# Hybrid attention layer: in its second attention half, three PSUM banks for scores and three for transposes, in place of two and four

## What is computed

```python
rel = jax.nn.relu(jnp.einsum('bqhd,bkd->bqhk', qib, k_idx) * (D_IDX ** -0.5))
score = jnp.einsum('bqhk,bqh->bqk', rel, wib)
score = jnp.where((s[None, :] <= t[:, None])[None], score, -jnp.inf)
_, idx = lax.top_k(score, k_top)
...
logits = jnp.einsum('bqhd,bqkhd->bhqk', qb, kg) * (D_HEAD ** -0.5)
logits = jnp.where(sel_ok[:, None], logits, -jnp.inf)
p = jax.nn.softmax(logits, axis=-1)
return jnp.einsum('bhqk,bqkhd->bqhd', p, vg)
```

## Time and profile before

| | us |
|---|---|
| median of 3 executions | 1729.43 |
| lowest, highest | 1728.17, 1732.9 |
| the profiled execution | 1732.58 |
| its span, first to last instruction | 1730.8 |

### The profile page before, as it was taken

One profiled execution on the slowest core, in us unless ns is written; L12 is line 12 of the kernel. 1 busy time (PEld: TensorE's weight loads), 2 busy tenths in 40 slices (PEclk: granted clock), 3 DMA queues, 4 the chain that ended last, 5 costly groups with the idle time before them and its releaser, 6 DMA issues. The chain is left out here.

```text
span 1730.8 us, 23456 instructions
## 1 busy us (share of the span) xinstructions
PE 1633.7 (94%) x8360; PEld 1376.5 (80%) x8360; DVE 1240.2 (72%) x1966; ACT 853.1 (49%) x1650; POOL 546.6 (32%) x332
## 2 busy tenths in 40 slices
PE   5999999999999999988889999899999989999997
PEld 5899888799877777777768878688888878888885
DVE  6287798898988989688863445874554458777878
ACT  5366455455445545577751243655555543333334
POOL 1111245555435435321103450675555500000000
PEclk9999999999999999999989999999999999999998
DMA  4565424344333233356304352233444365443544
GB/s 177 171 184 152 123 94 141 114 127 114 95 101 107 93 106 107 102 126 135 87 28 156 134 183 98 97 140 140 164 168 159 118 237 201 158 170 122 171 140 103
DMA packets 101372, 231.23 MB, mean 134 GB/s; under 512 B 11192, under 2 KB 25848, under 8 KB 101256
## 3 DMA queue, kind: packets, MB, share of 16 engines
q1 hardware_dynamic: 100680, 227.64, 41.2%
q0 software_dynamic: 576, 2.10, 0.7%
HBM read 155.83 MB, written 73.86 MB: 133 GB/s over the span
## 5 line engine op out<-in xcount | busy, mean ns | idle before, releaser
L727 PE MATMUL pj<-x_hi,w_hi 128*128 128x512 f32 (+2 forms) x816 | 304.0, 373 | 1.8 <-DVE rp_t L1031 1.8
L727 PE MATMUL pj<-x_lo,w_hi 128*128 128x512 f32 (+2 forms) x816 | 294.0, 360 | 0.0
L727 PE MATMUL pj<-x_hi,w_lo 128*128 128x512 f32 (+2 forms) x816 | 293.9, 360 | 0.0
L683 POOL TENSOR_TENSOR pt_lo<-a_buf,pt_hi 128x512 fp32r<-128x512 f32 (+3 forms) x104 | 137.5, 1338 | 191.0 <-ACT pt_hi L948 191.0
L336 POOL TENSOR_TENSOR w_lo<-w_raw,w_hi 128x1024 fp32r<-128x1024 f32 x53 | 132.9, 2507 | 183.7 <-ACT w_hi L332 183.6
L1105 DVE TENSOR_SCALAR_CACHE_REDUCE counted<-sc,small 128x272 uint8<-128x272 f32 (+6 forms) x217 | 182.5, 891 | 0.9
L1693 PE MATMUL bank<-v_hi,f_hi 128*128 128x512 f32 x448 | 175.7, 392 | 4.0 <-DVE f_lo L2075 3.9
L1693 PE MATMUL bank<-v_hi,f_lo 128*128 128x512 f32 x448 | 175.4, 392 | 0.0
L1693 PE MATMUL bank<-v_lo,f_hi 128*128 128x512 f32 x448 | 175.2, 391 | 0.0
L727 PEld LDWEIGHTS pj<-x_hi,w_hi 128*128 128x128 f32 x816 | 156.3, 192 | 17.0 <-DVE rp_t L1031 2.1
L727 PEld LDWEIGHTS pj<-x_hi,w_lo 128*128 128x128 f32 x816 | 155.4, 190 | 17.8
(11 more groups left out here) (252 smaller groups left out, 3930.3 us busy)
## 6 DMA issues: line engine op xcount, KB each, us to landing
w_raw<-w_units SPq DMA_DIRECT2D x57, 512.0 KB, 3.7
f_raw<-f_d SPq DMA_DIRECT2D x28, 1024.0 KB, 5.0
u_raw<-w_units SPq DMA_DIRECT2D x32, 512.0 KB, 4.6
f_d<-f_s SPq DMA_DIRECT2D x64, 256.0 KB, 2.2
b<-w_units SPq DMA_DIRECT2D x16, 1024.0 KB, 7.8
f_d<-c SPq DMA_DIRECT2D x48, 256.0 KB, 2.2
k_hi<-k_d SPq DMA_DIRECT2D x32, 260.0 KB, 5.6
k_lo<-k_d SPq DMA_DIRECT2D x32, 260.0 KB, 6.2
```

The lines of the kernel that those rows point to most:

```text
L683: pool.tensor_tensor(pt_of(pt_lo, j, tiles), raw, pt_of(pt_hi, j, tiles).bitcast(F32), ALU.subtract).then_inc(sb_lo, 1)
L727: mm = pe.matmul(pj[b][:, 0:c1 - c0], w[:, s, kt, :], a[:, kt, c0:c1], start=kt == 0 and k == 0, stop=kt == KT - 1 and k == 2)
```

## The change

The transposes keep the ring (4, 5, 6) to the end, three banks where there were four from step 66 on. Bank 0 goes to the scores: from chunk NZ_SB on (the first of step 64) the chunks go round (2, 3, 0). Z_BANK is the bank of each chunk and Z_PREV the chunk that last held it. The waits of `scores` follow from Z_PREV: in the second half a chunk waits for the chunk three back; the first chunk in bank 0 waits for the last projection chunk there, number 102 of 104. The readers of the scores use Z_BANK. Nothing else differs: the same instructions in the same order on each engine, with other banks and other semaphore values.

```diff
-    ring = (4, 5, 6) if j < NJ // 2 + 2 else (4, 5, 6, 0)
+    ring = (4, 5, 6)
...
+Z_BANK = [2 + z_ % 2 if z_ < NZ_SB else (2, 3, 0)[(z_ - NZ_SB) % 3] for z_ in range(Z_END[-1])]
+Z_PREV = [max([y_ for y_ in range(z_) if Z_BANK[y_] == Z_BANK[z_]], default=None) for z_ in range(Z_END[-1])]
...
-                        if 2 <= z < NZ_SB + 2:
-                            pe.wait_ge(zs_used, z - 1)
-                        elif z >= 2:
-                            pe.wait_ge(zd_used, z - 1 - NZ_SB)
-                        dst = bk[2 + z % 2][:, 0:c1 - c0]
+                        if z >= NZ_SB and Z_BANK[z] == 0 and Z_PREV[z] is None:
+                            bank_read(NC_ALL - 2 + NC_ALL % 2)
+                        elif Z_PREV[z] is not None and Z_PREV[z] < NZ_SB:
+                            pe.wait_ge(zs_used, Z_PREV[z] + 1)
+                        elif Z_PREV[z] is not None:
+                            pe.wait_ge(zd_used, Z_PREV[z] + 1 - NZ_SB)
+                        dst = bk[Z_BANK[z]][:, 0:c1 - c0]
...
-                        src = bk[2 + z % 2][:, 0:c1 - c0]
+                        src = bk[Z_BANK[z]][:, 0:c1 - c0]
...
-                        dve.tensor_tensor_reduce(n_buf[:, s, c0:c1], bk[2 + z % 2][:, 0:c1 - c0], mask,
+                        dve.tensor_tensor_reduce(n_buf[:, s, c0:c1], bk[Z_BANK[z]][:, 0:c1 - c0], mask,
                                                  -DH ** -0.5, last, ALU.add, ALU.min, out).then_inc(zd_used, 1)
```

## The result

| | kernel before | changed kernel |
|---|---|---|
| median of 4 executions, us | 1729.76 | 1748.61 |
| lowest, highest | 1728.17, 1732.9 | 1742.95, 1751.7 |
| the profiled execution, its span | 1732.58, 1730.8 | 1751.7, 1749.9 |

The ratio of the times is 1.0101, with a 95% interval of 1.0082 to 1.0119. By the medians the change makes the kernel 18.9 us slower, where 4.2 had been forecast. Its executions also spread more: 8.8 us from lowest to highest, against 4.7.

The account below looks back on a forecast made before the run. The prediction took a dependence relay between VectorE and TensorE's products as the bound. Terms 2.6 + 0.45 + 1.0 + 0.5 - 0.35 = 4.2 us on the median 1729.43 gave 1733.6 us, range 1728 to 1741 for 8 in 10.

Parts of the forecast that it names:

- The path: Second attention half: VectorE's work and TensorE's products alternate, four legs; a change is worth what it does to them.
- The third score bank gains nothing, within a few tenths: Score chunks: VectorE has no idle time when the third chunk comes; gain 0.05 us in 7 heads, 0.35 us.
- The sum for the lost transpose bank: Second half: 2.6 + 0.45 + 1.0 + 0.5, less 0.35 for the score bank, 4.2 us slower.
- (a): Step 4 of a head without sums: second values group waits, nine-slot product 0.65 us later, four times, 2.6 us.
- (b): Step 4 of a head with sums (84, 100, 116): first sums group waits longer, 0.15 us each, 0.45 us.
- (c): Step 1 of a head, seven steps: a single transpose gets between release and product, 0.14 us each, 1.0 us.
- (d): Step 129: the second group of the last sums starts later, moving the end of the stage by 0.5 us.
- the clock rival: Gathered TensorE idle time at (a), (b), (c) drops the clock; about 1738 to 1742 us, chance 0.25.
- The price of a drop: Seven-slot product and first score pair behind it, 16 matmuls, each about 0.1 us longer: 1.6 us a drop.
- The fourteen waits that were priced at 22 us together: Clock rival's upper case: if the steps of (a), (b) and (c) all drop, 14 x 1.6 = 22 us more.

Follow-up runs that it names:

- e11: Kernel before with three score and four transpose banks, products in bank 7 alone, 12 unread matmuls ahead of the seven-slot product: 1733.10 us.
- e2: Changed kernel with unread matmuls at both long waits, 12 before step 1's single transpose and 10 before the second values group: 1734.77 us.
- e5: Changed kernel with 12 unread matmuls only before the single transpose of step 1: 1734.87 us.
- e10: Changed kernel with unread matmuls at step 1 (12), before the second values group (10) and in the last two waits (10 and 16): 1728.12 us.
- e4: Kernel before with 8 and 16 unread matmuls in TensorE's last two waits of the half, step 129: 1722.66 us.
- e7: Kernel before with one wait more: the second values group of the second half waits for the group three back: 1734.81 us.
- e8: Kernel before with one wait more: the single transpose of step 1 waits for the group three back: 1729.18 us.
- e1: Kernel before with the transposes on three banks, still two score banks, bank 0 unused: 1739.29 us.
- e12: Changed kernel with 4 unread matmuls, not 12, ahead of the single transpose of step 1: 1745.81 us.
- e3: Kernel before with three score banks and four transpose banks, all second-half products in bank 7: 1741.94 us.
- e9: Kernel before with unread matmuls in the last two waits (10 and 16) and the two waits of step 65 (4 and 13): 1721.19 us.

## Why the prediction was wrong

**The path** was right. Between TensorE and VectorE the relay is as told; the third chunk comes sooner and VectorE takes it in its turn. VectorE's third chunk in the changed kernel starts at 742.80, 1.86 us behind TensorE's, where before it was 0.82 (743.56 and 742.74). **The third score bank gains nothing, within a few tenths**: right on a ring of four (e11, 10.44 against 10.43 us a head), a little low on a ring of three, 1 us in place of 0.35.

**The sum for the lost transpose bank** was near: 4.2 us, against 5.0 in e2, 4.4 in e5 and 5.5 in e10 against e4. Its terms: (a) was mis-sized, 0.84 us a step in e7 in place of 0.65. After a wait the four small transposes take 0.36 us (755.76 to 756.15 is 0.39 in the changed kernel), not the 0.20 of a running stream. (b) was 0.15 a step. The leg over values and sums is 783.19 - 770.86 = 12.33 in e7, against 780.89 - 768.69 = 12.20 before, 0.13, but e7 has only a part of it; in e10, which has it whole, it is 783.67 - 771.21 = 12.46 against 781.32 - 769.11 = 12.21 in e4, 0.25. (c) was 0.14 a step; e8 shows 0.28, twice that, for the same reason as in (a): behind its wait the single transpose takes 0.26 us up to the product (744.62 to 744.88). With the 0.15 that the third score bank gives back, 0.08 a head are left in e10. (d) was 0.5: from VectorE's last block 4 chunk to the first matmul of L346 it is 14.16 us in e10 and 13.77 in e4, 0.39. Added up with (a) as e10 has it (10.96 against 10.19 us, 0.77), that is 3.1 + 0.75 + 0.6 + 0.4, or 4.8 us, for the 4.2 of the sum; (a) and (b) make the difference.

**The step that failed** is that the forecast priced the gathered idle time of TensorE at nothing. Its sum takes the clock as held through the waits of (a), (b) and (c), and what a drop costs stood only in the clock rival, with a chance of 0.25, mostly for a few drops. In place of that the changed kernel ran some 37 us of the half at 1.2 GHz, in eight stretches, and this cost 15.5 us in its profile and 13.8 by the medians of the changed kernel and e2. The rival had named the places and the signs; it is what happened. Three things went into that. First, the idle time at step 1 was put at 1.2 to 1.5 us by adding the two waits. It was 1.75, and one reason is that TensorE also gained shorter delays ahead of them: from the transposes of step 71 to the first chunk of step 72 it took 0.69 us before (740.30 to 740.99) and 0.35 now (739.31 to 739.66). Second, the one row that spoke against it (1.12 us of idle time and no drop) was given more weight than the one that spoke for it (1.55 and a drop), though the new waits lay on the side of the second. Third, I took each drop by itself, as a few in fourteen; with waits of this length in every head, 8 of the 14 were followed by one.

The price of a drop was estimated at 1.6 us. From the first block 6 chunk of the half to its last block 4 chunk, the changed kernel took 906.28 - 724.00 = 182.28 us and e2 891.77 - 725.01 = 166.76, by VectorE's start times. The 15.5 us between them belong to some 37 us at the low clock: 0.4 us lost for each microsecond at half speed, so that most of what TensorE did there was on the path. The changed kernel's profile is of the slowest of its four executions, that of e2 is near its median, which is why this is more than the 13.8 us between the medians. The eight stretches between make 1.9 us each. The fourteen waits that were priced at 22 us together gave these 15.5.

The rule of the Trainium skill (Perfetto Trace Analysis, section Matmul Optimizations), that matmuls should run back to back since the engine scales its power with its use, was set against my forecast, and the runs agree with its direction: e2 fills the waits and is 13.8 us faster. The rule of the Trainium skill (Perfetto Trace Analysis, section Matmuls) that independent matmul groups should rotate through different PSUM banks speaks for either use of bank 0. As a third bank for the scores it gave 0.15 us a head at a held clock (e10 against e1), and taken from the transposes it cost more than that.

## What to carry to other kernels

A wait of TensorE that costs nothing can still be worth keeping: with two short ones the clock held, and with one long one it fell. Where TensorE waits for another engine in a fixed rhythm, look at what a change does to its longest idle time, not only to its total, and give a drop of the clock an even chance or so (8 of 14 waits here) once that idle time comes near the length behind which the same trace shows one. The forecast should hold a price for it. And where it must wait for over a microsecond ahead of matmuls on the path, matmuls that nobody reads are cheap: 24 of them in two places took 7 us off this kernel.

## What the runs showed of the hardware

No fixed length of idle time divides drop from no drop. In e12 1.28 us at step 73 went by without one and 1.29 us at step 81 brought one, in the same place of the pattern. In e5 a values' wait of 1.74 us (step 84) went by without one; in e12 the same wait, 1.73 us, was followed by one. In e1 the values' wait of step 84, only 1.08 us, was followed by one, where 1.12 us in the kernel before and 1.17 in e7 at the same step were not. Nor do the executions of one program agree: the four of e12 took 1742.69, 1744.88, 1746.74 and 1747.96 us at mean clocks over the whole kernel of 0.982, 0.978, 0.976 and 0.973, and of the changed kernel's four the fastest (1742.95) had 0.980, the others 0.971 to 0.973. Where in the kernel their low clock lay is known for the profiled execution alone. This goes with the wide spread of the changed kernel (1742.95 to 1751.7) and of e3; e10, without a low clock between 740 and 905 us in its profile, spread only from 1726.73 to 1728.92 over eleven executions. At the end of the half, the profiled executions of before and e8 had some 14 and some 10 us of it. What decides in a single case is not settled by these runs.

Work that nobody needs made three kernels faster: e2 against the changed kernel by 13.8 us, e4 and e9 against the kernel before by 7.1 and 9.4.
